# Decay exponents from running-sum rows, and the transposed corner block on VectorE, in a gated-delta and window-attention layer

## What is computed

```python
gc = jnp.cumsum(scal_chunks(g), axis=-1)
decay = jnp.exp(jnp.where(lower, gc[..., :, None] - gc[..., None, :], -jnp.inf))
n_mat = jnp.where(strict, -jnp.einsum('nbhid,nbhjd->nbhij', kb, kc) * decay, 0.0)
t_mat = jnp.eye(CHUNK, dtype=f32) + n_mat
for _ in range(int(math.log2(CHUNK)) - 1):
    p_mat = jnp.einsum('nbhij,nbhjk->nbhik', p_mat, p_mat)
    t_mat = t_mat + jnp.einsum('nbhij,nbhjk->nbhik', t_mat, p_mat)
qk = jnp.einsum('nbhid,nbhjd->nbhij', qc, kc) * decay
```

## Time and profile before

| | |
|---|---|
| median of 3 runs | 2640.78 us (2640.4 to 2642.45) |
| profiled execution, its own time | 2643.21 us |
| span of its instructions | 2641.3 us |
| PE busy | 2607.7 us, 99% |
| DVE busy | 1340.7 us, 51% |
| ACT busy | 893.8 us, 34% |
| POOL busy | 400.1 us, 15% |
| DMA queue of the weights | 45.5% of 16 engines' span |

### The profile page before, as it was taken

The page is one execution under the profiler, slowest core; times in us unless marked ns, Lnnn a source line. Parts: engine busy times, 40 slices in busy tenths (PEclk is TensorE's granted clock), DMA queues, the critical chain, the costliest instruction groups (busy, mean ns, idle before and its releaser), DMA issues.

```text
span 2641.3 us, 50170 instructions
## 1 busy us (share of the span) xinstructions
PE 2607.7 (99%) x20320; PEld 2140.7 (81%) x20320; DVE 1340.7 (51%) x3442; ACT 893.8 (34%) x2870; POOL 400.1 (15%) x238
## 2 busy tenths in 40 slices
PE   7999999999999999999999999999999999999998
PEld 6877887788888888888888888888888888888887
DVE  6677777223266666612336666651223666665022
ACT  4454544422244334321114344432112334434101
POOL 3433343343210110000000011000000011000000
PEclk9999999999999999999999999999999999999999
DMA  7555455687643333355563333335545333333554
GB/s 249 190 198 179 170 180 195 248 280 290 245 167 120 127 128 121 129 193 217 179 224 127 121 130 131 131 114 207 209 177 221 133 116 131 132 116 128 200 213 175
DMA packets 78997, 458.41 MB, mean 174 GB/s; under 512 B 13232, under 2 KB 17456, under 8 KB 31792
## 3 DMA queue, kind: packets, MB, share of 16 engines
q1 hardware_dynamic: 65664, 427.85, 45.5%
q10 hardware_dynamic: 13104, 27.36, 3.0%
HBM read 352.42 MB, written 102.76 MB: 172 GB/s over the span
## 4 chain that ended last, share of the span: by engine, by line
PE 91%; DVE 5%; POOL 1%; DMA 1%; issue 1%; ACT 1%; POOLq 0%; DVEq 0%; SPq 0%; ACTq 0%
PE bank L1296 24%; PE bank L1298 23%; PE bank L1297 23%; PE last_banks L1418 3%; PE last_banks L1406 2%; PE bank L1484 1%; PE bank L1394 1%; PE bank L1469 1%; PE bank L1461 1%; PE bank L1530 1%; PE last_banks L1539 1%; PE bank L1520 1%; PE bank L1515 1%; PE last_banks L1536 1%; PE bank L1476 1%
## 5 line engine op out<-in xcount | busy, mean ns | idle before, releaser
L1296 PE MATMUL bank<-hT_hi,w_sl 128*128 128x512 f32 x2112 | 890.0, 421 | 0.0
L1298 PE MATMUL bank<-hT_hi,w_sl 128*128 128x512 f32 x2112 | 827.5, 392 | 0.0
L1297 PE MATMUL bank<-hT_lo,w_sl 128*128 128x512 f32 x2112 | 826.6, 391 | 0.0
L1298 PEld LDWEIGHTS bank<-hT_hi,w_sl 128*128 128x128 f32 x2112 | 396.8, 188 | 87.0
L1296 PEld LDWEIGHTS bank<-hT_hi,w_sl 128*128 128x128 f32 x2112 | 398.1, 188 | 77.1 <-issue 1.0
L1297 PEld LDWEIGHTS bank<-hT_lo,w_sl 128*128 128x128 f32 x2112 | 399.0, 189 | 59.2 <-issue 0.7
L437 POOL TENSOR_TENSOR w_sl<-w_raw,w_sl 128x1024 fp32r<-128x1024 f32 x90 | 218.7, 2434 | 347.6 <-ACT w_sl L518 337.6
L975 DVE SCALAR_TENSOR_TENSOR area<-zraw,stc,area 128x512 f32<-128x512 f32 x288 | 219.7, 763 | 3.3
L456 POOL TENSOR_TENSOR gu<-mk,g_hi 128x512 fp32r<-128x512 f32 x32 | 45.9, 1436 | 644.4 <-DVE nmx L1092 605.2
L1139 DVE SCALAR_TENSOR_TENSOR s_cur<-s_cur,scs,last_banks 128x128 f32<-128x128 f32 x112 | 38.9, 347 | 206.0 <-PE last_banks L1536 206.0
L612 ACT ACTIVATE area<-area 128x512 f32<-128x512 f32 x96 | 60.5, 630 | 218.7 <-DVE area L975 218.7
(11 more groups left out here) (242 smaller groups left out, 4259.6 us busy)
## 6 DMA issues: line engine op xcount, KB each, us to landing
w_sl<-saved_w SPq DMA_DIRECT2D x270, 1024.0 KB, 4.8
saved_w<-w_sl SPq DMA_DIRECT2D x90, 1024.0 KB, 4.9
w_raw<-in_w_tiles SPq DMA_DIRECT2D x90, 512.0 KB, 5.9
area<-in_x ACTq DMA_DIRECT2D x4, 2048.0 KB, 9.6
area<-in_x ACTq DMA_DIRECT2D x14, 512.0 KB, 7.5
out_y<-area ACTq DMA_DIRECT2D x3, 2048.0 KB, 7.3
bias_sb<-in_bias ACTq DMA_DIRECT2D x32, 128.0 KB, 2.2
out_y<-area SPq DMA_DIRECT2D x4, 512.0 KB, 2.7
```

The source lines that it names most:

```text
L1296: pe.matmul(dst, a_hi, b_hi, start=first, stop=False)
L1297: pe.matmul(dst, a_hi, b_lo, start=False, stop=False)
L1298: return pe.matmul(dst, a_lo, b_hi, start=False, stop=last)
```

## The change

The exponents are no longer made by products. In the prologue PE makes, beside the three sums, the running sums of each half chunk as rows (a product whose output is heads by positions) and one correction column group. ACT copies the rows out, writes them to a DRAM buffer `sum_rows` of 32x128, and PE turns them back into columns (`turn_sums`), which ACT copies to `sums_at`. For each head ACT issues a DMA that spreads that head's 4 rows over all 128 partitions (`load_row`, 256 KB written). POOL subtracts the column value from the row (`exponent`), and adds a mask of 0 or -3e38. ACT takes the exponential from there. Since the lower part is then zero already, `dec_u` is not made. The transposes of `tt` on PE and ACT's copy of the corner are gone: DVE transposes four 32x32 blocks per chunk straight from `tt` to `od`. The masks that are loaded at the start grow from 5 to 8 (320 KB to 512 KB).

```diff
@@ POOL
             def decays(h, n1):
-                pool.wait_ge(sc_ready, n1)
-                pool.wait_ge(g_split, (n1 - 1) // H + 1)
-                for up, g in zip(g_up, (g_hi[:, :, :].bitcast(F32), g_lo[:, :, :])):
-                    ins = pool.tensor_tensor(up, mk[:, UPTO:UPTO + 1, :].to_broadcast([P, NT, P]),
-                                             g[:, :, h, None].to_broadcast([P, NT, P]), ALU.mult)
-                ins.then_inc(gup_ready, 1)
+                pool.wait_ge(row_moved, row_moves(n1))
+                pool.wait_ge(ecums, 2 * ((n1 - 1) // H + 1))
+                after(pool, dec_ready, n1 - 1)
+                pool.tensor_tensor(exponent[:, :, :].rearrange("p t (a c) -> p t a c", a=2),
+                                   sums_row[:, :, :].rearrange("p t (a c) -> p t a c", a=2),
+                                   sums_at[:, :, :, h, None].rearrange("p a t o -> p t a o").to_broadcast([P, NT, 2, CH]),
+                                   ALU.subtract).then_inc(row_read, 1)
+                pool.wait_ge(row_read, n1)
+                pool.tensor_tensor(exponent[:, :, :], exponent[:, :, :], mk[:, MASKED:MASKED + 1, :].to_broadcast([P, NT, P]),
+                                   ALU.add).then_inc(gup_ready, 1)
@@ ACT, prologue
-                act.wait_ge(cums, b1)
+                act.wait_ge(cums, 2 * b + 1)
                 act.activation(sc_all[:, EGC:ETAIL + 1, :, :].rearrange("p q t h -> p (q t h)"),
                                bank[7][:, 0:3 * NT * H], ACT.Exp).then_inc(ecums, 1)
+                act.activation(sums_at[0:CH, 1, :, :].rearrange("p t h -> p (t h)"), bank[7][0:CH, 3 * NT * H:4 * NT * H], ACT.Copy)
+                act.activation(sums_t[:, :], bank[7][0:NT * H, P:2 * P], ACT.Copy).then_inc(rows_ready, 1)
+                act.wait_ge(rows_ready, b1)
+                act.dma_start(sum_rows, sums_t[:, :]).then_inc(row_moved, 16)
+                yield
+                act.wait_ge(cums, 2 * b1)
+                sums_col = bank[7][:, 2 * P:2 * P + NT * H]
+                act.activation(sums_at[:, 0, :, :].rearrange("p t h -> p (t h)"), sums_col, ACT.Copy)
+                act.activation(sums_at[CH:P, 1, :, :].rearrange("p t h -> p (t h)"), sums_col[CH:P], ACT.Copy).then_inc(ecums, 1)
+                load_row(b, 0)
@@ ACT, project of every head but the first of a block
+                if h:
+                    load_row(b, h)
@@ ACT, head
-                act.wait_ge(dec_done, n1)
-                act.activation(dec, bch(5), ACT.Exp).then_inc(dec_ready, 1)
+                act.wait_ge(gup_ready, n1)
+                act.activation(dec, exponent[:, :, :], ACT.Exp).then_inc(dec_ready, 1)
@@
-                act.wait_ge(ft_done, n1)
-                act.activation(od[CH:P], bch(5)[CH:P, :, 0:CH], ACT.Copy).then_inc(merge_act, 1)
@@ DVE, head
-                ch.inc(dve.tensor_tensor(dec_u, dec, mk[:, UPTO:UPTO + 1, :].to_broadcast([P, NT, P]), ALU.mult))
@@
+                def turned_corner():
+                    for a in BLOCKS[0:2]:
+                        for c in BLOCKS[2:4]:
+                            ins = dve.transpose(od[c, :, a], tt[a, :, c])
+                    ins.then_inc(od_ready, 1)
@@
                 attention()
+                turned_corner()
                 fill(1)
                 quotient(0)
@@ PE, prologue
-                for i, m in enumerate((UPTO, ONES, AFTER)):
-                    ins = pe.matmul(bank[7][:, i * NT * H:(i + 1) * NT * H], mk[:, m, :], gs, start=True, stop=True)
-                ins.then_inc(cums, 1)
+                for i, m in enumerate((UPTO, ONES, AFTER, HALF_REST)):
+                    pe.matmul(bank[7][:, i * NT * H:(i + 1) * NT * H], mk[:, m, :], gs, start=True, stop=True)
+                pe.matmul(bank[7][0:NT * H, P:2 * P], gs, mk[:, HALF_UPTO, :], start=True, stop=True).then_inc(cums, 1)
+
+            def turn_sums(b):
+
+                pe.wait_ge(rows_ready, b + 1)
+                pe.transpose(bank[7][:, 2 * P:2 * P + NT * H], sums_t[:, :], ident[0:NT * H, 0:NT * H]).then_inc(cums, 1)
@@ PE, head
-                pe.wait_ge(gup_ready, n1)
-                pe.matmul(bank[5][:, :], after_r[:, :], g_up[0].rearrange("p t c -> p (t c)"), start=True, stop=False)
-                pe.matmul(bank[5][:, :], after_r[:, :], g_up[1].rearrange("p t c -> p (t c)"), start=False, stop=True
-                          ).then_inc(dec_done, 1)
                 transposes(1, k)
@@
-                pe.wait_ge(dec_ready, n1)
-                pe.wait_ge(f_ready, n1)
-                for t in range(NT):
-                    ins = pe.transpose(bch(5)[:, t, :], tt[:, t, :], ident)
-                ins.then_inc(ft_done, 1)
                 logits_padded()
```

More of the change, by code:

```diff
@@ L768, in _ @@
             next(pro)
+            next(first)
+            next(first)
+            next(pro)
             for _ in first:
```

77 lines of the change are left out of this document (44 added, 33 removed).

## The result

The changed kernel takes 2656.42 us (median of 5 runs, 2653.34 to 2663.51) where the kernel before takes 2640.78. The ratio is 1.0059, with a 95% interval of 1.0048 to 1.007: slower by 0.6%, and outside the range of the prediction. Its granted clock of TensorE is 0.991 of full speed in the mean; the other four have 0.995 or 0.996, and the kernel before 0.999.

The account below looks back on a forecast made before the run. PE, busy in 99% of the span, was taken as the bound. Terms -13.4 - 2.7 + 4.0 + 2.4 + 0.8 = -8.9 us from the median 2640.78 gave 2631.9 us (chance 0.40), range 2624.5 to 2641.

Parts of the forecast that it names:

- The price of the transposes: DVE, between attention and the quotient: four transposes at 0.24 us, 0.96 us in all, bounds 0.7 and 1.2.
- The slack: Blocks 1 to 3: DVE has 0.70 us to spare at apply(2), so 21 heads gain 0.64 us each, 13.4 us.
- Removed work: PE: two products, 0.47 us, and four transposes, 0.43 us, go; 0.90 us in each of 32 heads.
- Block 0: Heads 1 to 6: 0.35 us gained at the logits, DVE's chain 0.96 longer, 0.61 us later; whole block +4.0 us.
- Head 0 of block 0 comes out even: First head of block 0: -0.90 us and +0.96 on DVE, where it already is just in time.
- the rows' way to DRAM and back costs nothing: Prologues: extra ACT copies and the DMA to DRAM and back lie under four tiles of the last projection, no cost.
- Prologues and start: Prologues: 0.6 us each (bounds 0.3 and 1.0), +2.4 us over four; start: larger constants +0.8 us (bounds 0 and 1).
- Dearer transposes: Rival on DVE: transposes at 0.30 us each, 1.20 us, costing 6.5 us more over 27 heads; 2638.4 us, chance 0.18.
- The tie in block 0: Rival: POOL's low part starts after L1045, which takes 0.16 us; 0.7 us better in 6 heads, 2627.7 us, chance 0.15.
- POOL's pair: Rival: POOL's new pair ends late and holds up DVE's L971, PE waiting in 28 heads; 2671 us, chance 0.06.
- Swallowed: Rival: PE arrives earlier and waits for kd, f or DVE everywhere, as in block 0; 2641 us, chance 0.09.

Follow-up runs that it names:

- spread: The changed kernel with one DVE transpose each behind level(2), level(3), level(4) and diagonal(), none behind attention(): 2623.85 us, ratio 0.9938.
- spread_late_row: The kernel of spread with ACT's issue of the next head's row transfer moved behind the first conv_in and refill: 2626.61 us, ratio 0.9948.
- busy_wait: The changed kernel with six throwaway PE products of 512 columns in block 0 before probs(0): 2647.98 us, ratio 1.0028.
- rows_only: The changed kernel with the four transposes back on PE and the corner's copy back on ACT, keeping the running-sum rows: 2638.11 us, ratio 0.999.
- under_pool: The changed kernel with DVE's four transposes issued one instruction group earlier, ahead of the small operation held behind POOL's low part: 2637.86 us, ratio 0.999.

## Why the prediction was wrong

**The price of the transposes** is the first step that failed: "I take 4 x 0.24 = 0.96 us, since operations on DVE overlap in this way everywhere in the trace". They took 1.28 us, above the upper bound of 1.2. Rows 7 show an operation that covers all partitions; those here each go to another quarter, and are held. That operations on DVE overlap everywhere in the trace was wrong: the four copies at 810.68 us don't, and the rival's argument that starts in another quarter are not in the trace was wrong with it. The fixed term of the Trainium skill ("VectorE: DVE Perf Modes", section on the TRN2 errata), measured there on additions of two tensors, gave an estimate of 1.16 us and pointed the right way. The Trainium skill's rule on the quarters, on the same page, would have given one whole duration each, an estimate of 4 x 0.30 = 1.20 us by rows 8, near the truth, and I had not used it.

**The slack.** "DVE has 0.70 us to spare" was read at `apply(2)` alone, and nearly right. Four transposes cost a head of block 1 (360.4 - 355.3) / 7 = 0.73 us, two cost (355.9 - 355.3) / 7 = 0.09: with 1.28 and 0.64 us of work, a room of 0.55 in both. Of the 0.73 us 0.53 are in front of `apply(2)`; most of the rest is in front of `probs(0)`, which starts 14.81 us behind the first k with k in the changed kernel and 14.64 in *spread*. The prediction had left 0.3 us in hand there; the quotient ends at 830.02, and PE takes it at 830.08. By its own formula, with the measured terms, the step reads 21 x (0.96 - 1.28 + 0.55) = 4.8 us of gain in place of 13.4; in the profiled executions these heads gained 5.4. The structure was right, and 21 heads multiplied an error of 0.32 us in the price and 0.15 in the slack.

**Removed work.** "Together 0.90 us in each of 32 heads" was nearly right: 0.49 with the rows alone (forecast 0.47), 0.96 with both where nothing is late.

**Block 0** was put at +0.61 us a head: 0.35 us gained at the logits, 0.96 lost behind them. The logits were right: they start 8.34 us behind the head's first k with k (8.20 before), which itself comes 0.47 us earlier in the head, so 0.33 are gained. But "DVE's chain starts 0.35 earlier" carries nothing to the quotient. What stands ahead of that is the end of POOL's low part, 203.56 - 188.8 = 14.8 us behind the first k with k, and 194.32 - 179.9 = 14.4 before: of the gain 0.1 us is left. What is missing goes to the third DMA that ACT issues ahead of its rounding of the next weight: with it moved away (*spread_late_row*) `probs(0)` comes 0.23 us earlier. Behind that end the transposes count with their whole 1.28 us, so a head takes 54.17 us at full clock (*busy_wait*) against 52.93 before: +1.24 and not +0.61. Where they stand elsewhere (*spread*) it takes 52.79, 0.14 less than before.

"Head 0 of block 0 comes out even" failed too, and with it that the rows' way to DRAM and back costs nothing: POOL waited 1.4 us for the row in the changed kernel and 4.0 in *rows_only*, and by *rows_only* head 1 begins 2.7 us later than before, where 1.4 was forecast for everything ahead of it. In the changed kernel it is 6.2 us in the profiled execution, with two falls of the clock of 6.8 us each in it.

**The clock** was not in the prediction at all, neither as a term nor as a rival. It makes about 8 of the 24.5 us by which the median was missed. Without it the kernel would still be slower than before and outside the range (*busy_wait*, 2647.98). Every row that I read stood at full clock, so nothing in the trace of the kernel before showed what a wait of 2 us sets off; that such a thing was possible could be seen at 50 to 56 us, the one place outside the span's end where it fell, which I had not looked at.

**Prologues and start.** The last head of block 1 and the prologue of block 2 together take 290.7 us, from the first product of k with k in the one to the first behind the other, against 290.55. Since the head is 0.9 us shorter, the prologue is 1.1 us longer, where 0.6 was forecast with 1.0 as upper bound: some 2 us more over the four, if the first is like the others. The constants' wait is 11.80 against 11.19 us, the 0.6 forecast as 0.8. Beyond that the start varies: the first k with k stands at 77.7 us in the changed kernel, but at 73.5 in *busy_wait*, whose code is the same up to there, and at 75.1 before.

**The rivals.** Dearer transposes came true, and more dearly: 0.32 and not 0.30. The tie in block 0 didn't: L1079 started 0.27 us behind POOL's low part and was caught in full. POOL's pair, the only slow case that I had (2671), was innocent at 2.67 us. Swallowed came true in part: in a head of block 1 PE lost 0.73 of the 0.96 us again, waiting for DVE and not for `kd`. About half of the 15.6 us by which the kernel became slower, the clock's, comes from a mechanism that I gave no chance. The sum of the miss: 9.3 us in blocks 1 to 3, and 15.2 in the start, block 0 and the prologue of block 1, of which about 8 are the clock's. The first number is from the profiled executions, the rest is what the median leaves.

## What to carry to other kernels

Before work is moved to an engine that is idle half of the time, find in which of its waits it is to lie: the same change made this kernel 16 us slower with its four instructions in front of a result that TensorE waits for, and 17 us faster with them in waits behind it. Small VectorE operations that go from one quarter of the partitions to another didn't overlap in any row here; count their whole duration, and look for a group of that kind in the trace, even of another operation. And where a change makes TensorE's waits longer, look at the granted clock behind the longest of them, since what follows may run at half of it for several microseconds. And compare the granted clock of the profiled execution with that of the other runs before its numbers are taken for the typical ones.

## What the runs showed of the hardware

- TensorE, busy in 98% of the span, still fell to 1.2 GHz for 3.4 or 6.8 us behind single waits of 2.0 us, and in some heads behind waits of 1.2 to 1.7 us. With waits of 0.5 to 0.7 us in the same place it didn't.
- Six products without a use in each head of block 0, issued into a wait, made a kernel 8.4 us faster in the median.
- A VectorE transpose of 32 by 128 elements takes 0.304 us, as long as one of 128 by 128 from SBUF; two in a row start 0.32 us apart if they change the quarter of the partitions, and 0.24 if they don't. Copies of that size that change the quarter follow one another 0.01 us behind the end, too.
- Such transposes, issued while GpSimd's subtraction of 128 by 1024 elements ran, kept their 0.32 us (*under_pool*); a VectorE operation of 4 elements per partition issued 0.27 us behind its start took 2.15 us and ended with it.
- A fall of the clock can't be seen in the page's row of tenths over 67 us slices; windows of 2 us show it.
